# A decoder step on one core: the value gathers of PEER consumed four tokens at a time, and four more cached-key iterations placed inside the value phases

## The reference, cut to what matters

```python
u = peer_u[expert]
act = jax.nn.gelu(jnp.einsum('thkd,td->thk', u, xb))
return jnp.einsum('thk,thkd->td', gate * act, peer_v[expert])
```

```python
s = s + jnp.einsum('bqhd,bshd->bhqs', q, k_all)      # 4096 cached positions per sample
o = jnp.einsum('bhqs,bshd->bqhd', softmax(s), v_all)
```

## Time and profile before

| | |
|---|---|
| median of 3 runs | 2939.2 us (2935.93 to 2942.57) |
| span of the profiled execution | 2941.5 us |
| PE busy | 2043.5 us (69%) |
| DVE busy | 1178.5 us (40%) |
| POOL busy | 1142.2 us (39%) |
| ACT busy | 419.2 us (14%) |
| moved by DMA | 774.45 MB, 263 GB/s over the span |

### The profile page before, as it was taken

The page is one execution under the profiler, slowest core; times in us unless marked ns, Lnnn a source line. Parts: engine busy times, 40 slices in busy tenths (PEclk is TensorE's granted clock), DMA queues, the critical chain, the costliest instruction groups (busy, mean ns, idle before and its releaser), DMA issues.

```text
span 2941.5 us, 34786 instructions
## 1 busy us (share of the span) xinstructions
PE 2043.5 (69%) x11577; PEld 866.0 (29%) x11577; DVE 1178.5 (40%) x2742; ACT 419.2 (14%) x803; POOL 1142.2 (39%) x1076
## 2 busy tenths in 40 slices
PE   6778877367868977774889677739694434432898
PEld 1444556245622223331232233312121111100222
DVE  2333452957446034444700444457503222224161
ACT  2323332000101012221010122211000000000100
POOL 0000000346463643333736545467752222225573
PEclk8778898676879987886999788869895555555998
DMA  4000041377597989898989898989698999998996
GB/s 170 15 16 8 9 166 44 149 273 267 189 384 277 371 314 316 298 323 284 340 301 364 295 324 311 316 269 335 247 399 303 337 325 328 328 331 297 327 341 241
DMA packets 254182, 774.45 MB, mean 263 GB/s; under 512 B 36514, under 2 KB 45371, under 8 KB 250763
## 3 DMA queue, kind: packets, MB, share of 16 engines
q0 software_dynamic: 150784, 547.43, 51.5%
q1 hardware_dynamic: 102138, 221.64, 21.5%
q10 hardware_dynamic: 1168, 4.23, 0.4%
HBM read 766.36 MB, written 6.81 MB: 263 GB/s over the span
## 4 chain that ended last, share of the span: by engine, by line
PE 33%; DMA 30%; DVE 15%; issue 11%; POOL 5%; another core or an unknown queue 4%; ACT 2%; SPq 0%; POOLq 0%; DVEq 0%; ACTq 0%
DMA arena<-peer_u,eidx 26%; PE ps L1397 13%; PE ps L1241 6%; DVE arena L1090 5%; PE ps L1351 4%; POOL arena L453 4%; DMA arena<-peer_v,idxT 3%; PE ps L1295 1%; PE ps L1310 1%; PE ps L1336 1%; PE ps L1433 1%; PE ps L1285 1%; PE ps L1303 1%; POOL arena L463 1%
## 5 line engine op out<-in xcount | busy, mean ns | idle before, releaser
L453 POOL DMA_INDIRECT arena<-peer_u,eidx x512 | 548.9, 1072 | 1409.7 <-DVE acc L1090 737.2
L1090 DVE CUSTOM_DVE_ANT_0 arena<-arena 128x1024 f32<-128x1024 f32 x512 | 625.0, 1226 | 962.5 <-DMA arena<-peer_u,eidx 945.2
L1397 PE MATMUL ps<-arena 128*32 128x512 f32 x2048 | 710.9, 623 | 64.2 <-DMA arena<-peer_v,idxT 55.2
L453 POOL DMA_INDIRECT arena<-peer_v,idxT x512 | 539.4, 1054 | 338.7 <-PE ps L1397 242.3
L1433 PE MATMUL ps<-arena 128*128 128x512 f32 x512 | 322.8, 740 | 124.6 <-DMA arena<-kpe_pool 120.8
L1397 PEld LDWEIGHTS ps<-arena 128*32 128x32 f32 x2048 | 177.0, 112 | 580.4 <-issue 365.2
L1513 PE MATMUL ps<-arena 128*32 128x512 f32 x512 | 123.8, 1057 | 237.6 <-DMA arena<-vn_pool 236.8
L664 ACT ACTIVATE arena<-ps 128x512 f32<-128x512 f32 x256 | 152.2, 598 | 811.4 <-PE ps L1433 489.3
L1351 PE MATMUL ps<-hb,arena 128*128 128x128 f32 x1024 | 154.7, 308 | 49.7 <-issue 44.3
L1241 PE MATMUL ps<-arena 128*128 128x512 f32 (+3 forms) x400 | 175.5, 600 | 7.9 <-DVE arena L886 7.5
L1351 PEld LDWEIGHTS ps<-hb,arena 128*128 128x128 f32 x1024 | 142.9, 219 | 62.7 <-issue 55.4
(11 more groups left out here) (294 smaller groups left out, 1646.1 us busy)
## 6 DMA issues: line engine op xcount, KB each, us to landing
arena<-kt_pool SPq DMA_DIRECT2D x256, 320.0 KB
arena<-vn_pool SPq DMA_DIRECT2D x256, 320.0 KB
arena<-w_q SPq DMA_DIRECT2D x16, 1024.0 KB, 13.5
arena<-w_in SPq DMA_DIRECT2D x8, 1236.0 KB, 15.6
arena<-w_o SPq DMA_DIRECT2D x16, 512.0 KB, 6.9
arena<-peer_u,eidx POOLq DMA_INDIRECT x512
arena<-peer_v,idxT POOLq DMA_INDIRECT x512
hb<-x_prompt SPq DMA_DIRECT2D x8, 512.0 KB
```

Of the source, the lines that this page charges most:

```text
L453: pool.indirect_dma_start(ring[:, q % RING, :], None, table, bass.IndirectOffsetOnAxis(ap=index, axis=0)).then_inc(g[q % RING], 16)
L1090: V_.tensor_tensor_reduce(ring[:, q % RING, :], ring[:, q % RING, :], xn2[:, b, :], 1.0, 0.0, ALU.mult, ALU.add, acc[:, k:k + 1]).then_inc ...
L1397: last = T_.matmul(ps[32 * j:32 * j + 32, i, :], W32[:, j, c, :], ring[:, q % RING, 512 * i:512 * i + 512], start=(c == 0), stop=(c == 31) ...
```

## The change

Two things change.

First, `v_phase` goes through the tokens in groups of four. PE waits for the four gathers of the group, then issues half 0 of its four tokens, one in each column group, then half 1 of all four, and then raises `v_used` by 4 at once. A `between` entry at any k of a group runs before the group.

Second, the bounds of the loops move, on PE and on ACT alike. Value phase 0 now holds iterations 0, 1 and 2 (before tokens 40, 64 and 88), u phase 1 has iterations 3 to 8 beside it (six, it had seven), value phase 1 holds 9, 10 and 11 (before tokens 24, 56 and 88; it had one), and u phase 2 has 12 to 15 beside it (four, it had seven). On ACT `gate_exp(1)` and `gate_exp(2)` come behind the last of them.

```diff
@@ ACT
-            decode_scores(0, 1)
+            decode_scores(0, 3)
             gate_exp(1)
             store_y(0)
-            decode_scores(1, 8)
+            decode_scores(3, 9)
             gelu(1)
             load_h(1)
-            decode_scores(8, 9)
+            decode_scores(9, 12)
             gate_exp(2)
             store_y(1)
-            decode_scores(9, 16)
+            decode_scores(12, 16)
@@ PE, v_phase
-                for k in range(P):
-                    q = 2 * P * b + P + k
-                    c, j = k // 4, k % 4
-                    if k in between:
-                        between[k]()
-                    pe.wait_ge(g[q % RING], 16 * (q // RING + 1))
+                for c in range(P // 4):
+                    for k in range(4 * c, 4 * c + 4):
+                        if k in between:
+                            between[k]()
+                    q = 2 * P * b + P + 4 * c
+                    for j in range(4):
+                        pe.wait_ge(g[(q + j) % RING], 16 * ((q + j) // RING + 1))
                     for i in range(2):
-                        last = T_.matmul(ps[32 * j:32 * j + 32, i, :], W32[:, j, c, :],
-                                         ring[:, q % RING, 512 * i:512 * i + 512], start=(c == 0), stop=(c == 31),
-                                         tile_position=(0, 32 * j), skip_group_check=True)
-                    last.then_inc(v_used, 1)
+                        for j in range(4):
+                            last = T_.matmul(ps[32 * j:32 * j + 32, i, :], W32[:, j, c, :],
+                                             ring[:, (q + j) % RING, 512 * i:512 * i + 512],
+                                             start=(c == 0), stop=(c == 31),
+                                             tile_position=(0, 32 * j), skip_group_check=True)
+                    last.then_inc(v_used, 4)
@@ PE, calls
-            v_phase(0, {16: turn_decode_queries, 24: absorb_decode_queries, 40: first_scores})
+            v_phase(0, {16: turn_decode_queries, 24: absorb_decode_queries, 40: first_scores,
+                        64: lambda: decode_scores(1, 2), 88: lambda: decode_scores(2, 3)})
...
-            decode_scores(1, 8)
+            decode_scores(3, 9)
...
-            v_phase(1, {40: lambda: decode_scores(8, 9)})
+            v_phase(1, {24: lambda: decode_scores(9, 10), 56: lambda: decode_scores(10, 11),
+                        88: lambda: decode_scores(11, 12)})
...
-            decode_scores(9, 16)
+            decode_scores(12, 16)
```

## The result

The changed kernel takes 3185.9 us (median of four runs, 3176.3 to 3191.7), the kernel before 2940.9 on the same chip (2935.9 to 2960.2). The ratio is 1.080, with an interval from 1.075 to 1.085. I forecast 3078 us, with a range from 3004 to 3160. The direction is the forecast's; the loss is 245 us where I had 139.

The account below looks back on a forecast made before the run. It took PE to set value phases 0 and 1 before, and a serial ring circle after. Value phases +71, +68, +12, +9 and u phases -21 sum to +139 us: 3078 us, range 3004 to 3160.

Parts of the forecast that it names:

- groups, v0 and v1: Value phases 0 and 1: 16 circles, 197 us, with one stay and the small transposes, against 219 us now.
- groups, v2 and v3: Value phases 2 and 3: tokens at 1.54 instead of 1.43 us outside phase 2's softmax stretch; +12 and +9 us.
- stays, two more in each of v0 and v1: Value phases 0 and 1: each iteration placed there takes PE some 35 us without tokens and costs the phase 30 us.
- a quick pass through the full ring behind the stay: After a stay PE takes both landed groups in 5.8 us instead of 12.3; 5 us of that is kept.
- a circle of 12.3 us: Value phases: serial loop of slot release, three gather-start steps, the fourth gather and PE's matmuls takes 12.3 us per 8 tokens.
- The fourth gather: Value phases: a group's last gather takes 5.4 us from start to PE's use, between 5.1 with few under way and 6.6.
- C: PE's time for a group of four tokens: 1.9 us at full clock, 3.6 at half, 2.9 expected from a mixture.
- my 184 us for a phase without stays: Kernel before, value phases 0 and 1: 219 us less a stay of 35 leaves 184 for 128 tokens, 1.43 us each.
- So PE does set them: Kernel before, value phases 0 and 1: PE's token work, 1.37 us each, and the stay add up to the phase's length.
- the faster rival: PE was the bound and DMA takes over, so stays cost nothing beside gathers: -83 us, 2856 us; chance 0.06.
- all at half clock: Rival: every group takes PE 3.6 us and stays last 38 us; +202 us, 3141 us; chance 0.20.
- the gathers keep up: Rival: fourth gather usable within 4.5 us, clock stays up, circle near 10.2 us; +18 us, 2957 us; chance 0.08.

Follow-up runs that it names:

- group_only: Kernel before with the new `v_phase` in groups of four but the old loop bounds; ratio 1.059 (1.052 to 1.066).
- stays_only: Kernel before with the new loop bounds but the old `v_phase`, tokens one by one; ratio 1.036 (1.028 to 1.044).
- no_stays: Kernel before with iterations 0 and 8 moved from value phases 0 and 1 to u phases 1 and 2; ratio 0.974 (0.967 to 0.982).
- ring4_old_order: Kernel before with waits and release by four, each token's two matmuls still together; ratio 1.053 (1.043 to 1.062).
- half the work: Kernel before without half 1 of the tokens' matmuls, except the first and last four tokens of each value phase; ratio 0.990 (0.986 to 0.994).
- skew_old: Kernel before with half 0 of each token issued ahead of half 1 of the previous one, waits and releases one by one; ratio 1.002 (1.001 to 1.004).

## Why the prediction was wrong in size

By the prediction's own terms, in us. The parts of the group are read from group_only less the kernel before, those of the stays from the changed kernel less group_only. The first row holds what the forecast wanted back from the one stay that was there already, since group_only has it too.

| term | forecast | measured |
|---|---|---|
| groups, v0 and v1 | 197 + 30 + 3 - 219 = +11, +8 | +35, +40 |
| groups, v2 and v3 | +12, +9 | +32, +30 (+35, +33 in the changed kernel) |
| stays, two more in each of v0 and v1 | +60, +60 | +55, +50 |
| u phases 1 and 2 | -5, -16 | -3, -14 |
| all before v0; u phase 3; behind the table's v3 | 0 | -10, +11, +3 |

The direction was right, and the u phases to 2 us each, which is less than profiles of one kernel differ by. The stays were 5 and 10 us under their terms. A stay lasts 32 to 35 us and costs 25 to 29: stays_only gives 29 and 27 each in phases 0 and 1, the changed kernel less group_only 28 and 25. PE's timeline around the first stay of stays_only shows both the loss and what the ring gives back:

```profile
891.79 1.98 PE L1433 MATMUL ps<-arena 128*128 128x512 f32 x4
...
926.33 3.68 PE L1397 MATMUL ps<-arena 128*32 128x512 f32 x32
934.37 23.09 PE L1397 MATMUL ps<-arena 128*32 128x512 f32 x64 [4.37 <-DMA arena<-peer_v,idxT]
```

34.5 us without a token, then 8 tokens at once, then 4.4 us in which the ring is empty: 8.0 us for 8 tokens that else take 11.4, so 3.4 of the 34.5 come back at once.

In the changed kernel the forecast's way of getting 5 us back, a quick pass through the full ring behind the stay, did not come. The 8 tokens behind its third stay take 3.64 us (1068.47), but the next group starts at 1082.90, 14.4 us later, no sooner than a circle. What is saved stands ahead of the stay: PE would have waited some 7 us for the next group, and is at work on the stay instead. That is my reading of the rows, and 34 less 7 fits the 25 to 28 us. So the price of a stay was right with a wrong mechanism, which is luck.

The groups were the miss: +40 forecast, +136 measured. That is 96 us, as much as the 94 by which the profiled span missed its own sum (3174.5 - 2941.5 = 233, against 139); the other rows, -15 for the stays among them, nearly cancel.

**The step that failed** is "a circle of 12.3 us". It measured 13.82, and 16 circles of 1.52 more are 24 us a phase, where the groups' terms fell short by 24, 32, 20 and 21. Two parts of the circle were too small:

- The fourth gather, of which I took 5.4 us from its start to PE's use: 6.03 in the chain above and 0.14 more to PE's first instruction; 6.05 and 5.95 in group_only. I placed it between the ends of the earlier trace rows nearer to the quiet one, expecting only few gathers under way. In this stretch POOL starts eight in a row, so the fourth of a half has others beside it; that this makes it slow is argued, not shown. +0.8 us.
- C, of which I took the mean of a mixed clock, 2.9. The mixture came (0.64 in value phase 2, 0.67 in 3), but it is no mixture along the chain. Where the groups alternate, the chain passes through the slow one, behind the long wait; elsewhere both are slow. A mean over both groups is the wrong number for a chain through one of them. +0.8 us. The Trainium skill, "TensorE: Matmul & The Clock Gate", section "HAM oscillation — how this bites in real kernels", says that short bursts between waits for DMA each start cold; the rows agree for all 52 bursts behind 4 us or more (3.3 to 3.64 us), not for the 25 behind shorter waits that took 1.92, and for the sum the cold ones alone counted.

One cost was in no term: after the transpose that opens a phase PE now waits for the fourth gather, not the first (6.3 us in value phase 1). Some 3 to 5 us on the other side was my 184 us for a phase without stays, which is 187 to 189 (no_stays).

```profile
1479.84 0.47 PE L1384 MATMUL ps<-con,acc 128*128 128x128 f32 x1 [86.82 <-DVE acc L1094]
1486.57 3.59 PE L1399 MATMUL ps<-arena 128*32 128x512 f32 x16 [6.26 <-DMA arena<-peer_v,idxT]
```

**A step that was wrong and did little harm to the sum** is "So PE does set them". I took 1.37 us for a token's matmuls from 26.07 us for 19 tokens, and that a group of four "now needs 5.5". PE's row is one stretch of overlapping instructions that runs on as long as the next token lands before the last has ended; it says how fast tokens came, not how fast PE could go. What PE needs for eight landed tokens, 3.68 us, stood in the earlier trace rows, and I used that row for the end of the stay only. The Trainium skill, "TensorEngine Tiling (Array Packing)", section "Theoretical Speedup", allows a factor of up to 4 for 32 columns; ring4_old_order shows that the old order has it already: 4 tokens in 1.95 us, where one alone takes 1.90. Read rightly, that row takes away the ground of the faster rival, in which PE was the bound.

Of the rivals, "all at half clock" was nearest, at 3141: its C of 3.6 is what the chain has. It kept the gather at 5.4 us, and its stays of 38 us did not come (32 to 35).

One reading of the rows was wrong too, against the rival "the gathers keep up": "no row of the chain is that short", 4.5 us from a gather's start to its use. The chain of the kernel before has such rows of `peer_u`, the same 512 KB, with two or three gathers under way: 4.13 us at 2651.74, 4.36 at 1940.63. In the value phases of the changed kernel none was under 5.0 us, so it did no harm.

What stays open: why POOL's gather starts in the kernel before are 1.44 us apart in some stretches (955.95, 957.39), each released by PE, and 1.24 to 1.28 in others. With half the work or with skew_old they are at 1.24 to 1.28, and the whole kernel gains 1% or nothing. No run changed the number of slots, so that a deeper ring would take the circle away is not tested.

## What to carry to other kernels

Before reordering matmuls to let the array's column groups work side by side, find a row in which several inputs had already landed: if PE was fast there, the order isn't what holds it. In a ring of few slots, waiting for several at once or releasing several at once turns overlapped fetches into one serial circle; write it out with the duration of the gather under the load that the new pattern makes, and with PE's time at the clock that the chain's own group will have, not a mean. And work that is only put between fetches costs nearly its full length when the ring holds a fraction of it: here 8 slots gave back 5 to 9 of some 34 us, and moving the last such work out gained between 1 and 3%.

## What the runs showed of the hardware

- Matmuls of 32 columns run side by side over different column groups even when a token's own instructions stand together: 16 in 1.95 us at 2.4 GHz and 3.67 at 1.2, where 4 in one group alone take 1.90 and 3.62 (ring4_old_order; the earlier trace rows).
- With a periodic wait of 7 us and one of 1.4 to 1.8 us, the groups run at 1.2 GHz behind the long wait and at 2.4 behind the short one, for several circles in a row. In other stretches, with waits of 2.4 to 3.9 us, all groups run at 1.2.
- A gather of 512 KB in the value phases of the changed kernel took 5.0 us or more from its start to use, 6.0 in the circle shown; beside the end of u phase 3 of the kernel before (2645 to 2664), with two under way, 4.1 to 4.5. The Trainium skill, "DMA: Bandwidth & Descriptors", section "Anatomy of one DMA — SWDGE (gpsimd) path", gives a fit of 2.0 us plus bytes at 436 GB/s, an estimate of 3.2 us. With the 0.94 us of the start, which these durations include, that is an estimate of 4.1: the rows with two under way agree, those of the full ring do not.
